# Norms between matmul stages taken in two token halves

## What is computed

```python
h = h + 0.5 * swiglu(rmsnorm(h, ffn1_norm), w1, w3, w2)            # F1
q, k, v, u, g_attn, g_ssm = split(rmsnorm(h, mix_norm) @ w_in)      # u comes first: state space scan
h = h + (sigmoid(g_attn) * attn + sigmoid(g_ssm) * ssm) @ w_out     # merge, "wo"
h = h + 0.5 * swiglu(rmsnorm(h, ffn2_norm), ...)                    # F2
x = rmsnorm(h, final_norm)[:, 16:]
for i in (0, 1):                    # mixer: latent attention (i = 0), gated linear attention (i = 1)
    x = layer_norm(ALPHA * x + mixer(x), ln1_g[i], ln1_b[i])
    x = layer_norm(ALPHA * x + conv_ffn(x), ln2_g[i], ln2_b[i])     # C0, C1
    x = x + sigmoid(x @ ple_w_gate[i] + b[i]) * (p[i] @ ple_w_proj[i])   # "pg", "pp"
```

## Time and profile before

| | |
|---|---|
| median of three runs | 2974.54 us |
| the profiled execution | 2971.52 us |
| its span | 2969.5 us |
| TensorE busy | 2782.1 us, 94% |
| VectorE, ScalarE, GpSimd busy | 53%, 34%, 8% |
| mean granted TensorE clock | 0.968 |

### The profile page before, as it was taken

How to read it: one execution, slowest core, us unless ns; L and a number is a source line. 1 busy time by engine, 2 the same in 40 slices (tenths; PEclk the granted TensorE clock), 3 DMA queues, 4 the chain that set the end, 5 groups by cost and what they waited for, 6 DMA issues and landing times.

```text
span 2969.5 us, 33651 instructions
## 1 busy us (share of the span) xinstructions
PE 2782.1 (94%) x14075; PEld 2256.9 (76%) x14075; DVE 1570.1 (53%) x2370; ACT 1014.7 (34%) x1636; POOL 242.0 (8%) x246
## 2 busy tenths in 40 slices
PE   6999898999998999988999989999899978999988
PEld 5999898877687888875667668787678756878866
DVE  4653535656546433346655556557444365664744
ACT  3322223144334222233443344334333224433424
POOL 0233402010001000010000010000200001000020
PEclk8999999999999999999999999999999979999999
DMA  4332333421032222311111222323132202232312
GB/s 119 93 129 94 102 117 94 150 82 33 29 114 89 93 99 86 107 56 40 47 64 40 71 71 76 116 85 106 41 96 86 71 14 71 78 113 86 110 50 68
DMA packets 245517, 243.91 MB, mean 82 GB/s; under 512 B 19229, under 2 KB 238887, under 8 KB 245367
## 3 DMA queue, kind: packets, MB, share of 16 engines
q1 hardware_dynamic: 235527, 226.45, 23.7%
q0 software_dynamic: 5616, 13.22, 1.6%
q10 hardware_dynamic: 4224, 2.10, 0.2%
HBM read 230.70 MB, written 13.14 MB: 82 GB/s over the span
## 4 chain that ended last, share of the span: by engine, by line
PE 84%; DVE 10%; ACT 4%; issue 1%; DMA 0%; POOL 0%; SPq 0%; ACTq 0%; DVEq 0%; POOLq 0%
PE ps L541 24%; PE ps L542 24%; PE ps L543 24%; PE ps L1614 2%; PE ps L634 2%; PE ps L2021 2%; PE ps L2020 1%; DVE ul L529 1%; DVE rbuf L649 1%; DVE tmp L1911 1%; PE ps L2095 1%; ACT uh L518 1%; PE ps L1584 1%; PE ps L2067 1%; PE ps L1532 1%
## 5 line engine op out<-in xcount | busy, mean ns | idle before, releaser
L541 PE MATMUL ps<-XH,uh 128*128 128x512 f32 (+1 forms) x2424 | 889.0, 367 | 91.3 <-DVE XL L2217 28.7
L542 PE MATMUL ps<-XL,uh 128*128 128x512 f32 (+1 forms) x2424 | 882.8, 364 | 0.0
L543 PE MATMUL ps<-XH,ul 128*128 128x512 f32 (+1 forms) x2424 | 878.5, 362 | 0.0
L529 DVE TENSOR_TENSOR ul<-raw,uh 128x1024 fp32r<-128x1024 f32 (+3 forms) x416 | 520.4, 1267 | 550.1 <-ACT uh L518 549.9
L541 PEld LDWEIGHTS ps<-XH,uh 128*128 128x128 f32 x2424 | 466.7, 193 | 186.2 <-issue 68.4
L518 ACT CAST uh<-raw 128x1024 fp32r<-128x1024 f32 (+3 forms) x416 | 418.7, 1027 | 366.8 <-PE ps L543 363.2
L543 PEld LDWEIGHTS ps<-XH,ul 128*128 128x128 f32 x2424 | 467.0, 193 | 71.3
L542 PEld LDWEIGHTS ps<-XL,uh 128*128 128x128 f32 x2424 | 466.9, 193 | 70.6 <-issue 0.5
L541 PE MATMUL ps<-HH,uh 128*128 128x512 f32 (+1 forms) x880 | 308.5, 351 | 12.4 <-DVE HL L2292 11.4
L542 PE MATMUL ps<-HL,uh 128*128 128x512 f32 (+1 forms) x880 | 309.1, 351 | 0.0
L543 PE MATMUL ps<-HH,ul 128*128 128x512 f32 (+1 forms) x880 | 307.9, 350 | 0.0
(11 more groups left out here) (386 smaller groups left out, 3608.9 us busy)
## 6 DMA issues: line engine op xcount, KB each, us to landing
raw<-in_ffn_w SPq DMA_DIRECT2D x40, 1024.0 KB, 5.2
raw<-in_ffn_w_up SPq DMA_DIRECT2D x40, 1024.0 KB, 5.0
raw<-in_ffn_w SPq DMA_DIRECT2D x16, 1408.0 KB, 5.9
raw<-in_ffn_w_down SPq DMA_DIRECT2D x16, 1408.0 KB, 5.9
raw<-in_w_in SPq DMA_DIRECT2D x16, 1024.0 KB, 5.7
raw<-in_gla_w_in SPq DMA_DIRECT2D x12, 1024.0 KB, 5.1
raw<-in_mla_w_o SPq DMA_DIRECT2D x8, 1024.0 KB, 4.7
raw<-in_ple_w_gate SPq DMA_DIRECT2D x8, 1024.0 KB, 4.8
```

The source lines that it names most:

```text
L529: e.tensor_tensor(l, src, h.bitcast(F32), SUB).then_inc(*s_wlo.up(("unit", u)))
L541: e.matmul(o, wh, xh, start=first, stop=False)
L542: e.matmul(o, wh, xl, start=False, stop=False)
L543: return e.matmul(o, wl, xh, start=False, stop=last)
```

## The change

- **End of a stage.** Units 5, 6 and 7 of the last product run half by half (`lin_end`): token half 0 of 5, 6, 7, then half 1 of 5, 6, 7, with the column sums of half 0 put after units of half 1.
- **Start of a stage.** `lin_start` does half 0 of its first unit, then the column sum of half 1, half 0 of the second unit, and then half 1 of both, chunk by chunk. `lin_pair` stays for F1's start.
- Adds, squares, roots, reciprocals, centring and the splitting into high and low are issued per half (256 columns, 264 in B1), all of half 0 ahead of most of half 1. Products of the later stages read `XH2`, `XL2` (other memory), so that they can be written while the last product still reads its own.
- `feed_hi` and `feed_lo` get an argument `ahead`. The last unit of a stage and the first two of the next are fed with 0, and the feeds that stood behind them (c = 0 of a feed-forward, the head of the `u` and `cq` stages) go.
- A layer norm's bias is added inside the cast and the subtraction; `H` gets its bias in eight operations after both halves.
- `go` is added to `H` by VectorE straight from PSUM. ALPHA times `H` is done by GpSimd early in that stage.
- pg and pp run as pg, pg, pp, pp. `p[l]` is loaded, transposed and split during the feed-forward.

```diff
-        group = {"f1": 2, "c1": 2, "gs": 3, "pg": 2}.get(plan[i][0], 1)
+        group = {"f1": 2, "c1": 2, "gs": 3}.get(plan[i][0], 1)
...
+        def lin_end(e, name, X, halves, xs, keys, between):
+            us, (xh, xl, tag) = [], X
+            for hf, (t0, n) in enumerate(halves):
+                for j, key in enumerate(keys):
...
+                    i.then_inc(*s_mm.up(key + (hf,), *([("unit", us[j])] if hf else [])))
+                    if hf:
+                        between(j)
+
+        def lin_start(e, names, X, halves, keys, between):
...
+            for j, key in enumerate(keys):
+                us.append(next_unit(e, names[j]))
...
+                for k in range(8):
+                    s_lo.wait_ge(e, (tag, k, 0))
...
+                between(j)
...
+            for k in range(8):
+                s_lo.wait_ge(e, (tag, k, 1))
+                for u, key in zip(us, keys):
...
+        def rms_act(e, tag, halves, names, squared, X, y):
...
+            for k in LAST:
+                squared(k, 0)
+            squared(5, 1)
+            feed_hi(e, names[0], 0)
+            root(e, tag, halves, 1.0 / 1024, EPS6, hfs=(0,))
+            high(0)
+            squared(6, 1)
+            feed_hi(e, names[1], 0)
+            squared(7, 1)
+            root(e, tag, halves, 1.0 / 1024, EPS6, hfs=(1,))
+            high(1)
+
+        def rms_dve(e, tag, halves, names, add, X, y, src, gname):
...
+            for k in LAST:
+                add(k, 0)
+            add(5, 1)
+            feed_lo(e, names[0], 0)
+            inverse(e, tag, halves, hfs=(0,))
+            s_dv.wait_ge(e, NOW)
+            staged([piece(k, 0) for k in range(8)])
+            add(6, 1)
+            add(7, 1)
+            feed_lo(e, names[1], 0)
+            inverse(e, tag, halves, hfs=(1,))
+            s_dv.wait_ge(e, NOW)
+            staged([piece(k, 1) for k in range(8)])
...
         def ffn_act(...)
                     if c:
                         feed_hi(e, n1)
-                    else:
+                    elif not begun:
                         feed_hi(e, n3)
...
         def ssm_act(e):
-            feed_hi(e, "u")
             u_act(e, 0)
             u_act(e, 1)
             tables_act(e, 0)
...
+        def layer_start(e, tag, xt, names, keys):
+            layer_mean(e, tag, xt, 1)
+            lin_start(e, names, (XH2, XL2, xt), HB, keys, lambda j: layer_variance(e, xt, 1) if j == 0 else None)
+
+        def layer_dve(e, xt, i, which, names, add):
...
+            for k in LAST:
+                add(k, 0)
+            feed_lo(e, names[0], 0)
+            add(5, 1)
+            centre(0)
+            add(6, 1)
+            inverse(e, xt, HB, hfs=(0,))
+            s_dv.wait_ge(e, NOW)
+            staged([piece(k, 0) for k in range(8)])
+            add(7, 1)
+            feed_lo(e, names[1], 0)
+            centre(1)
+            inverse(e, xt, HB, hfs=(1,))
+            s_dv.wait_ge(e, NOW)
+            staged([piece(k, 1) for k in range(8)])
+
+        def layer_act(e, xt, i, which, names):
...
+            feed_hi(e, names[0], 0)
+            squares(0)
+            high(0)
+            feed_hi(e, names[1], 0)
+            squares(1)
+            high(1)
             for k in range(8):
+                s_lo.wait_ge(e, (xt, k))
                 e.activation(HV[:, k, :], HV[:, k, :], ACT.Identity, bias=...)
...
         def tail_pe(e, l):
...
+            for c in range(0, 8, 2):
+                for j in (c, c + 1):
+                    if j > 1:
+                        lin(e, "pg", x2, H2, ("pg", l, j))
+                    if l and j > 1:
+                        send_pe(e, j - 2)
+                for j in (c, c + 1):
+                    lin(e, "pp", (PPH, PPL, f"p{l}"), H2, ("pp", l, j))
```

More of the change, by code:

```diff
@@ L511, in feed_hi @@
             done["act use"] += 1
-            for u in range(done["act"], min(u + 2, len(units))):
+            for u in range(done["act"], min(u + 1 + ahead, len(units))):
                 x = units[u]
@@ L525, in feed_lo @@
             done["dve use"] += 1
-            for u in range(done["dve"], min(u + 2, len(units))):
+            for u in range(done["dve"], min(u + 1 + ahead, len(units))):
                 for j, (src, h, l) in enumerate(halves_of(u)[2]):
@@ new lines, in rms_act, with high @@
+        def rms_act(e, tag, halves, names, squared, X, y):
+            def high(hf):
+                t0, n = halves[hf]
+                for k in range(8):
+                    s_dv.wait_ge(e, (tag, "y", k, hf))
+                    e.copy(X[0][:, k, t0:t0 + n], y(k, hf)).then_inc(*s_hi.up((tag, k, hf)))
+            for k in LAST:
[9 more added lines that the diff above has]
+            high(1)
@@ L770, in setup_dve, with ffn_pe @@
             scaled("ffn1", (XH, XL), 8, T1, H, "ffn1")[1](e)
-        def ffn_pe(e, st, names, X, T, halves, side, param, before=None):
+        def ffn_pe(e, st, names, X, halves, spans, side, param, between, before=None, begun=True):
             n1, n3, n2 = names
@@ L797, in ffn_pe, with ffn_act @@
                 side.step()
-                for mm in range(2, 8):
+                for mm in range(2, 5 if grp else 8):
                     lin(e, n2, hid, halves, (st, "d", grp, mm), xs=xs)
                     side.step()
-        def ffn_act(e, st, names, halves, gate, down, side, param, before=None):
+            lin_end(e, n2, hid, spans, xs, [(st, "d", 1, k) for k in LAST], between)
+        def ffn_act(e, st, names, halves, gate, down, side, param, before=None, begun=True):
             n1, n3, n2 = names
@@ L825, in ffn_act @@
                 feed_hi(e, n2)
[L826 removed]
+                for mm in range(5 if grp else 8):
                     if mm > 1:
@@ new lines, in layer_pool, with layer_mean @@
+            for k in range(5):
+                add(k, (0, 512), (0, 1))
+            add(5, HB[0], (0,))
+            add(6, HB[0], (0,))
+            add(5, HB[1], (1,))
+            for k in (1, 2):
+                add_square(e, xt, k, HB[0], (0,))
+            add(6, HB[1], (1,))
+            for k in (1, 2):
+                add_square(e, xt, k, HB[1], (1,))
+        def layer_mean(e, tag, xt, hf):
+            colsum(e, xt + "m", [(accs[1], s_pool, (tag, "sum", 6)), (HV[:, 7, :], s_dv, (tag, 7))], HB, (hf,))
@@ new lines, in tail_act @@
+            none, side = Steps(), Steps()
+            side.add(input_act(e, l))
+            ffn_act(e, st, CONV, H2, conv_gate_act(l), no_down, side, none)
+            side.drain()
+            layer_act(e, f"x2{l}", l, 2, ("pg", "pg"))
+            for c in range(0, 8, 2):
+                for j in (c, c + 1):
+                    if j > 1:
+                        feed_hi(e, "pg")
+                    if l and j > 1:
+                        send_act(e, j - 2)
+                    if j > 2:
+                        s_dv.wait_ge(e, ("h2" if l == 0 else "h4", j - 3))
+                    s_dv.wait_ge(e, "hb")
+                    s_mm.wait_ge(e, ("pg", l, j, 0))
+                    e.activation(gate_tile(j), P(("pg", l, j, 0)), ACT.Tanh, scale=0.5,
+                                 bias=hb[:, 8 * l + j:8 * l + j + 1]).then_inc(*bk.free(s_fn, ("pg", l, j, 0), ("pg", l, j)))
+                for j in (c, c + 1):
+                    feed_hi(e, "pp")
```

600 lines of the change are left out of this document (363 added, 237 removed).

## The result

| | before | after |
|---|---|---|
| median | 2975.16 us (4 runs, 2971.31 to 2981.68) | 2998.23 us (4 runs, 2992.96 to 3001.08) |
| profiled execution, its span | 2971.52, 2969.5 us | 2992.96, 2991.1 us |
| mean granted TensorE clock | 0.968 | 0.968 |

The ratio is 1.0073, 95% interval 1.0050 to 1.0096: slower by 23 us. The forecast was 2999 us, slower. (That is the sum, +27, put on the profiled execution of 2971.52; put on the median of 2974.54 it would have been 3002.) The spans of the two profiles differ by 21.6 us. That this lies close to 27 is in part luck: two terms that the sum didn't have, -13 and +3, stand against borders that came out at +32.

The account below looks back on a forecast made before the run. The prediction took TensorE's chain, 84% of the span, as the bound, so its waits count. Border terms and +2.0 for transposes summed to +27 us on the profiled 2971.5, giving 2998.6, forecast as 2999 us; range 2972 to 3014.

Parts of the forecast that it names:

- B1: First rms border: pair over earlier, third `u` unit 9.1 us late behind the sine tables, a 2.33 us wait gone; -0.6 us.
- The late third units: At all seven borders the next stage's third unit is prepared late behind queued work; waits of 4 to 9 us, 45 together.
- the first rival: Halves hide the norms and the next unit isn't late: 2945 us if late starts sum to 15 or less; faster side 0.15.
- The add of unit 7 behind VectorE's pieces: Layer borders: this add is queued behind sixteen scalings and subtractions of half 0, so TensorE waits 6.1 us for the mean.
- B2: Rms border: pair over 2.4 us earlier, next unit's subtraction behind the 6.15 us positions block; +5.9 us with the clock.
- B3: Rms border with 11 chunks: pair over at 41.1 against 46.3, next unit at 45.0, restart at half clock; +0.8 us.
- B5 and B7: Layer borders with 11 chunks into pg and pp: late first pp unit and waits at pg/pp changes; +3.1 and +4.2 us.
- B4 and B6: Layer borders: pair over 1.8 us earlier at B4, third unit 6.5 us late, half clock; +6.6 and +5.1 us, transposes apart.
- The stages between the borders: Between the borders: no change in time, with one pitch of 0.23 us for all 512-column matmuls.
- GpSimd's half adds: Half adds taken at half of 2.14 and 1.29 us; rival: they cost as much as whole ones, 3016 us, within a shared 0.14.
- VectorE's and ScalarE's half operations: At the borders: pitches of 0.34 us for VectorE, 0.40 with a gain, 0.33 for ScalarE, 0.42 with a bias.
- The clock rival: Every wait over 0.35 us brings 4 us at half clock: +44, 3015 us; chance 0.14, shared with the GpSimd rival.

Follow-up runs that it names:

- experiments 1: The changed kernel with the third unit of each next stage cast and subtracted ahead of the second root at all seven borders: 2955.86 us, ratio 0.9923.
- 2 (made longer, +30): The changed kernel with eight more 512-column ScalarE copies in place behind the eight biases of each layer norm: 3028.22 us, ratio 1.0162.
- experiment 5: The changed kernel with third units fed ahead, half 1's add, centrings and squares before half 0's scalings, and both small units' subtractions before the first multiply-add: 2950.37 us.
- experiment 3: The changed kernel with only the add of unit 7, half 1, put ahead of half 0's scalings and subtractions at the four layer borders: 3009.70 us, ratio 1.0109.
- experiment 4: The changed kernel with half 1's add, centrings and squares ahead of half 0's scalings, and TensorE's second sum of squares ahead of the next stage: 2988.53 us.
- Experiments 9 to 11: Start of one low tile moved, each against an earlier follow-up kernel: hidden tile to a multiple of 512, 2929.56 us; input tile by 64 bytes, 2954.46; by 128, 2948.34.
- experiment 7: The kernel before with only the input of F2, C0, C1 and pg placed in tiles with rows 2048 bytes apart, not 2112: 2964.39 us, ratio 0.9954.

## Why the prediction was right, and where it wasn't

- **The late third units** ("Now ScalarE comes to it after eight biases"): right, 42.9 us against 45, each within 0.8 us. Shown by experiments 1 (taken away, -42) and 2 (made longer, +30). This is the term from which the first rival was to decide: its condition, late starts of 15 us or less, wasn't met by the changed kernel. Its 2945 lies near the kernels that have the cast ahead (2956, and 2950 with experiment 5), but with help: they have the 13 us of the placement in them, which neither the rival nor the forecast knew.
- **The add of unit 7 behind VectorE's pieces**: the wait is there, 5.84, 4.84, 5.84, 4.84 against 6.1 with eight chunks. But calling it a wait for the add misleads: experiment 3 gave the add its place and lost 11 us; experiment 4 moved the centrings as well and won 7 to 10.
- **B2**: right to 0.1 us, half 0 at a chunk's pace included. B3 0.9 off.
- **B5 and B7**: +2.5 and +5.2 against 3.1 and 4.2. The idle time at the changes between pg and pp was 3.5 us at B5, where 4.1 had been taken, and 6.4 at B7, where 5.6 had.
- **B4 and B6**: 9.2 and 6.4 against 7.6 and 6.1 with the transposes. At B4 the step that was mis-sized is the clock: the wait of 1.8 us ahead of the sum of squares was followed by the sum at full clock (17.0 to 19.6), and the lower level was taken behind longer waits only. The wait was 2.03, the sum of squares behind it ran at a granted clock of 0.58, and by the timeline it took 4.1 us (1736.74 to 1740.88), where 6 x 0.427 = 2.6 had been taken: 1.6 us.

```profile
1733.00:1736.00 3.00, 1.71 (x15) 1.00 0.00 0
1737.00:1740.50 3.50, 3.50 (x11) 0.58 0.02 5
1741.00:1744.00 3.00, 3.00 (x27) 1.00 0.00 0
```

(Stretch table: us, TensorE's busy time, clock, DMA.) The level is 2.4 GHz ahead of the wait and behind the sum, and near 1.2 between them. B6 has the same wait and the same 4.2 us (2494.81 to 2499.00); there the rest came out lower.
- **B1**: failed, +2.7 against -0.6. The step was "The wait of 2.33 ahead of the fourth unit goes." It did, but the stage isn't set by TensorE there: the sine tables, which now start later, carry their delay on. ScalarE's first sines come 4.1 us later than before (514.63 against 510.56), the next 4.9, the fourth pair 5.4. This is read from the traces; no experiment moved the tables.
- **The stages between the borders**: failed, -13 in place of 0. The change says that the later stages read other memory, and the prediction took that for a name. The rows to see it were those of XH and of other tiles at full clock; the sum took one pitch, 0.23, for all.
- **The working**: some terms don't follow from their own steps. B4's "before" has 19.9 where rows 5 give a gap of 19.6; the steps shown make B1 0.0, B3 +0.5, B5 +3.3 and B7 +4.8, not -0.6, +0.8, +3.1 and +4.2. With all of this the sum would be 28 to 29. The fixed part of a VectorE operation was read as 0.17 us from rows of 264 columns; with 0.41 at 256 and 0.69 at 512 it is 0.13. That GpSimd's scalings hold VectorE up by 0.3 us each stands on no row, and no run tested it; it isn't in the sum.
- **GpSimd's half adds**: the rival is out. All 40 cost 0.735 us, less than the half of 2.14 that was taken for the sums, a little more than the half of 1.29 for the squares.

```profile
L719 POOL TENSOR_TENSOR acc<-acc,tmp 128x256 f32<-128x256 f32 x24 | 17.6, 735 | 105.6 <-ACT tmp L709 104.5
...
L2370 POOL TENSOR_TENSOR acc<-acc,H 128x256 f32<-128x256 f32 x16 | 11.8, 735 | 47.7 <-DVE H L2551 27.5 <-DVE H L3008 10.1 <-DVE H L2294 10.1
```

- **VectorE's and ScalarE's half operations**: 0.41 and 0.48 us (L2416, L2421), and 0.51 with the bias (L2457), as taken (the pitches are about 0.09 less). The clock rival (+44) is out: most waits of 0.4 to 1.2 us leave durations of 0.39, full clock. But the assumption behind it and behind the sign "a wait above 2 us", that a wait's length alone decides, is wrong. The changed kernel has a wait of 1.06 us at B2, ahead of the sum of squares. In its first trace the clock stayed full behind it; in its second, of the same program, it was 0.50, and at the same place in those of experiments 1 to 4 it was 0.50 or 0.51. First and second trace:

```profile
937.60:940.60 3.00, 2.74 (x17) 1.00 0.05 16
```
```profile
941.00:944.00 3.00, 2.94 (x10) 0.50 0.04 9
```

What decides between the two isn't known.

## What to carry to other kernels

When a wait is cut by working in halves, list what each engine's queue holds between the last half and the next stage's third tile: that tile's preparation was hidden by the very gap that goes, and it has to be moved ahead of everything that waits for the pair. A wait names its releaser, not its cause: ask how long the releaser's list is up to that point, and whether moving the one instruction makes it shorter. And compare the pitch of the same instruction between tiles: where a tile starts is part of a change.

## What the runs showed that was not expected

**The start of the moving tile's rows.** 512 fp32r columns cost 0.2267 us a matmul with both tiles at a multiple of 512 bytes and rows 2048 bytes apart, and 0.2289 to 0.2320 in the other placements tried: 1 to 2.3% more for each matmul that reads them. Experiments 9 to 11, which move a start and nothing else, show that the start counts; experiment 7 shows what the placement is worth in all. The mechanism is open.

**The start of the kernel comes in two forms.** The first root stands at 31.1 to 32.3 us in five profiles of kernels with the same first instructions (31.81 in that of before), and at 34.6 to 35.0 in the other nine (34.96 in that of after). The difference is in the groups of transposes at the start, one per 1.26 us or, from about 18 us on, one per 0.75:

```profile
18.53 0.66 PE L741 MATMUL ps<-ident,xin 128*128 128x128 f32 x4
...
19.28 0.66 PE L741 MATMUL ps<-ident,xin 128*128 128x128 f32 x4
```
```profile
19.18 1.11 PE L863 MATMUL ps<-ident,xin 128*128 128x128 f32 x4
...
20.44 1.11 PE L863 MATMUL ps<-ident,xin 128*128 128x128 f32 x4
```

The clock goes with it. In the five traces the record of the granted clock begins, with 1.00, between 18.1 and 18.6 us; in the nine it begins between 32.4 and 34.8, behind all the transposes. (A stretch table prints 1.00 ahead of the first record too; nothing was measured there.) So 3.1 of the 21.6 us between the two profiles belong to no part of the change. The kernel of experiment 7, which has the start of before, shows the slow form too (34.83). Why the clock rises early in some executions and late in others isn't known.
